# The place of the Hyena norm's sum on TensorE and of its roots on ScalarE at the start of the attention loop

## Chip, cores and metric

One core of one Trainium2 chip. The time is device microseconds from launch to end; the profile adds a span, from the first to the last instruction. Engines: PE (TensorE), DVE (VectorE), ACT (ScalarE), POOL (GpSimd), SP (which issues the DMAs).

## What is computed

Two layers of a hybrid backbone over 256 latent tokens and 256 context tokens of width 1024. In each layer one input projection feeds three mixers: a bidirectional state-space scan, attention (8 query heads, 2 key heads, head size 64), and a Hyena long convolution. Each mixer's result gets an RMS norm of its own, the three stand side by side and go through an output projection; then follows a SwiGLU block. What matters here are the Hyena norm and the attention:

```python
def _rmsnorm(t, g):
    y = t * lax.rsqrt(jnp.mean(t * t, axis=-1, keepdims=True) + EPS)
    return y * g

def _gqa(q, k, v):
    s = jnp.einsum('bqgrd,bkgd->bgrqk', q, k)
    pr = jax.nn.softmax(s, axis=-1)
    return jnp.einsum('bgrqk,bkgd->bqgrd', pr, v)

y_hy = _rmsnorm(x0 * _long_conv(v * x1, filt, bias), hy_norm_g)   # 512 channels
x = x + g1 * (concat([y_ssd, y_att, y_hy]) @ w_out)
```

Layer 0 works on latent and context tokens (512 columns, 16 pairs of heads and token tiles), layer 1 on the latent tokens alone (256 columns, 8 pairs).

## The kernel before, in words

Each engine has an instruction list of its own, written out by hand; semaphores tie them together. `p.sig(ins, name)` counts a semaphore up when the instruction is done, `p.after(name, k)` waits on this engine for k more counts, `p.own(name)` for all that this engine itself has made. An engine works its list in order, so what stands behind a wait waits too. Features lie on partitions (blocks of 128), tokens on columns; most products are split into high and low halves (L716 to L718).

The Hyena result lies in `yhy` as four blocks. Its norm needs the sum over all 512 channels for each token:

1. ACT squares the four blocks into `fsq` (L1671).
2. POOL adds block 1 to 0 and block 3 to 2 (L608), and signals `hy_added` twice.
3. PE multiplies both sums with a matrix of ones and accumulates them in the PSUM bank `other + 1` (L1270): the sum over partitions, repeated on all of them. It signals `hy_summed` twice.
4. ACT makes the factor (mean + eps)^(-1/2) as an exponential of a logarithm into `hrs` (L1658, L1659) and signals `hy_rms`.
5. DVE multiplies the four blocks of `yhy` with `hrs` (L2359), ACT rounds them with the gain into `f_hi` (L1682, behind the copies of pairs 1 and 2), DVE makes the low halves `hy_lo` (L2351, ahead of the divisions of pairs 1 and 2), and from the fourth pair on PE uses them for the parts of the output projection (`part_half(PARTS + h)`).

At the same time the attention runs over pairs i, as a loop through three engines:

- PE: `scores(i + 1)` (L1194, into banks 4 and 5), `attend(i - 1)` (L1228, L1233), `turn_probs(i)` (transpositions, L1209, into banks 6 and 7).
- DVE: `invert_sums(i)` (L2283), `row_max(i + 1)` (L2275), `divide(i - 1)` (L2300, L2301), its half of `copy_probs(i)` (L2291). For i = 0 the multiplication of step 5 (L2359) stands behind the copy, with its wait for `hy_rms`.
- ACT: `softmax(i + 1)` (exponentials, L1645), its half of `copy_probs(i)` (L1654).

`scores(i + 1)` overwrites the banks of `scores(i)`, so it waits for both exponentials of pair i (L1192). `attend(1)` uses the bank of the Hyena sum and waits for `hy_rms` (L1217). Ahead of the loop stand `scores(0)` and two halves of a part of the output projection (`part_half(6)`, `part_half(7)`), then the sum (L1268 to L1270); on ACT `softmax(0)`, then the roots (L1673, L1674).

SP loads the weight pieces through a ring of four buffers; each load waits until PE has used the piece four places earlier (L450).

Of the kernel before, what the change touches and what calls it, by code (L numbers as in the profile page):

```python
# [108 lines left out]
def part_banks(l):  # L109

    parts = 2 * ((PLAN[l, "out"][1] - 2) % 2)
    return parts, 2 - parts


def half_after(l, i):


    h = (i - 3) // 2 if l == 0 and i % 2 == 1 else i - 3 if l == 1 else -1
    return h if 0 <= h < PARTS - 3 else None
# [116 lines left out]
def backbone(nc, x, c, ctx_in, c_ctx, w_mod, b_mod, norm1_g, w_in, ssd_conv_w, ssd_conv_b, ssd_a_log,  # L236
# [3 lines left out]
    with ExitStack() as stack:  # L240
# [3 lines left out]
        def at(name, kb, shape, dt=F32):  # L244
            return nc.alloc_sbuf_tensor_at(name, [P] + shape, dt, offset=base + int(kb * KB))
# [82 lines left out]
        prod, fsq = at("prod", 40, [2, 512]), at("fsq", 40, [4, T])  # L328
# [5 lines left out]
        hrs, ars = at("hrs", 180, [T]), at("ars", 182, [T])  # L334
# [5 lines left out]
        ps = stack.enter_context(nc.psum_tensor("ps", [P, 8, 512], F32))  # L340
        MOD, STAT, ACC = 4, 5, 5
        ident, ones, trif, trib = (c_sq[:, i, :] for i in range(4))
# [77 lines left out]
        def tokens(l):  # L420
            return T if l == 0 else L
# [201 lines left out]
        def _(pe):  # L623
            mm, transpose = nc.tensor.matmul, nc.tensor.transpose
            p = Program(pe, "pe")
# [247 lines left out]
            for l in range(DEPTH):  # L873
                n = tokens(l)
# [199 lines left out]
                for ch, (kind, col, idx) in enumerate(W_IN):  # L1074
                    if ch < 2:
                        continue
                    i, q, s = g0 + 2 * ch, q0 + ch, 2 * ch
# [54 lines left out]
                parts, other = part_banks(l)  # L1132
# [5 lines left out]
                def part_half(h):  # L1138


                    i, j = h // 2, h % 2
                    if j == 0:
                        pe.wait_ge(w_lo_done, g0 + i + 1)
                    if i > 0:
                        p.after("part_read")
                    else:
                        pe.wait_ge(pair_free[parts // 2], (q0 - 2) // 2 + 1)
                    last = block_of(g0 + i, parts // 2, j, 4, n, lambda k: mixed(i // 4, k), True, True)
                    if j == 1:
                        last.then_inc(w_used, 1)  # L1150
                    else:
                        p.sig(last, "part_half")

                def turn_vx(t):

                    if t >= 2:
                        p.after("vn_ready")
                    for k in range(4):
                        last = transpose(ps[:, 6 + t % 2, k * P:(k + 1) * P], halves[t % 2][:, k, t // 2, :], ident)
                    p.sig(last, "vx_transposed")  # L1160
# [24 lines left out]
                def scores(i):  # L1185


                    t, b = i // 4, i % 4
                    t0 = 0 if t < 2 else 2
                    for j in range(2):  # L1190
                        if i > 0:
                            p.after("probs_ready")  # L1192
                        row = slice(64 * j, 64 * j + 64)
                        last = mm(ps[:, 4 + j, 0:(4 - t0) * P].rearrange("p (t k) -> p t k", k=P), qkT[row, t, b, :],  # L1194
                                  qkT[row, t0:4, 4, :], start=True, stop=True)
                    p.sig(last, "scores")

                def turn_probs(i):


                    nk = 4 if i // 4 < 2 else 2
                    if i == pairs - 1:
                        p.after("probs_ready", 2)
                    for j in range(2):
                        if i > 0:
                            p.after(("probT_act", "probT_dve")[j])
                        for kk in range(nk):
                            keys = slice(kk * P, (kk + 1) * P)
                            last = transpose(ps[:, 6 + j, keys], prob[:, i % 2, j, keys], ident)  # L1209
                        p.sig(last, "turned_psum")  # L1210

                def attend(i):


                    nk, v0 = (4, 0) if i // 4 < 2 else (2, 2)
                    if i == 1:
                        p.after("hy_rms")  # L1217
                    if i >= 2:
                        p.after("o_ready")
                    if i == pairs - 1:  # L1220
                        p.after("probT_act")
                        p.after("probT_dve")
                    else:
                        pe.wait_ge(S["probT_act"], PAIRS_BEFORE[l] + i + 1)
                        pe.wait_ge(S["probT_dve"], PAIRS_BEFORE[l] + i + 1)
                    for kk in range(nk):
                        for j in range(2):
                            mm(ps[64 * j:64 * j + 64, other + i % 2, 0:P], v_nat[:, v0 + kk, j * HD:(j + 1) * HD],  # L1228
                               probT[:, i % 2, j, kk * P:(kk + 1) * P], start=(kk == 0), stop=(kk == nk - 1))
                    p.after("rec_ready")  # L1230
                    c = 2 * (i % 4)
                    for j in range(2):
                        last = mm(ps[64 * j:64 * j + 64, other + i % 2, P:2 * P], sm[:, 2, c + j:c + j + 1].to_broadcast([P, HD]), ident,  # L1233
                                  start=True, stop=True)
                    p.sig(last, "pv_done")

                pairs = 4 * tiles
                turn_vx(0)
                turn_vx(1)
# [25 lines left out]
                scores(0)  # L1265
                part_half(6)
                part_half(7)
                for k in (0, 2):  # L1268
                    p.after("hy_added")
                    p.sig(mm(ps[:, other + 1, 0:n], ones, fsq[:, k, 0:n], start=(k == 0), stop=(k == 2)), "hy_summed")  # L1270

                for i in range(pairs):
                    if i + 1 < pairs:
                        scores(i + 1)
                    if i > 0:
                        attend(i - 1)
                    turn_probs(i)
                    h = half_after(l, i)
                    if h is not None:
                        if h == 0:  # L1280
                            p.after("hy_ready", 4)
                        part_half(PARTS + h)
# [10 lines left out]
                for ch in range(4):  # L1293
                    i = g0 + PARTS + ch
# [20 lines left out]
                for part, (c0, cnt) in enumerate(FFN):  # L1315
# [12 lines left out]
                    for f in range(1 - part, cnt):  # L1328
                        for r in range(4):
                            up, half = gate_up(part, f, r)  # L1330
                            i, q = g0 + 4 * f + r, q0 + 2 * f + up
# [11 lines left out]
                    for ch in range(4):  # L1343
                        for sub in range(3):
                            i = g0 + 3 * ch + sub
# [33 lines left out]
        def _(act):  # L1379
            A = nc.scalar.activation  # L1380
            p = Program(act, "act")
# [90 lines left out]
            for l in range(DEPTH):  # L1472
                n = tokens(l)
# [159 lines left out]
                other = part_banks(l)[1]  # L1633
# [3 lines left out]
                def softmax(i):  # L1637

                    keys = T if i // 4 < 2 else L
                    if i >= 2:  # L1640
                        act.wait_ge(S["turned_psum"], 2 * (PAIRS_BEFORE[l] + i - 1))
                    for j in range(2):
                        c = 2 * (i % 4) + j
                        p.after("row_max")
                        p.sig(A(prob[:, i % 2, j, 0:keys], ps[:, 4 + j, 0:keys], ACT.Exp, bias=sm[:, 0, c:c + 1],  # L1645
                                accum_out=sm[:, 1, c:c + 1]), "probs_ready")

                def copy_probs(i):

                    keys = T if i // 4 < 2 else L  # L1650
                    act.wait_ge(S["turned_psum"], 2 * (PAIRS_BEFORE[l] + i) + 1)
                    if i >= 2:
                        act.wait_ge(S["pv_done"], PAIRS_BEFORE[l] + i - 1)
                    p.sig(A(probT[:, i % 2, 0, 0:keys], ps[:, 6, 0:keys], ACT.Copy), "probT_act")  # L1654

                def norm_features(sums, root, name):

                    p.chain(A(root[:, 0:n], sums, ACT.Ln, scale=1.0 / 512, bias=eps1[:, 0:1]))  # L1658
                    p.sig(A(root[:, 0:n], root[:, 0:n], ACT.Exp, scale=-0.5), name)  # L1659
# [10 lines left out]
                for k in range(4):  # L1670
                    p.sig(A(fsq[:, k, 0:n], yhy[:, k, 0:n], ACT.Square), "hy_sq")  # L1671
                softmax(0)
                p.after("hy_summed", 2)  # L1673
                norm_features(ps[:, other + 1, 0:n], hrs, "hy_rms")  # L1674
                for i in range(4 * tiles):
                    if i + 1 < 4 * tiles:
                        softmax(i + 1)
                    copy_probs(i)
                    if i in (1, 2):
                        for k in (2 * i - 2, 2 * i - 1):  # L1680
                            p.after("hy_normed")
                            p.sig(A(f_hi[:, 8 + k, 0:n], yhy[:, k, 0:n], ACT.Identity, scale=vecT[:, l, V_HYG + k:V_HYG + k + 1]), "hy_hi")  # L1682
                    h = half_after(l, i)
                    if h is not None and h % 2 == 1:
                        round_w(g0 + PARTS // 2 + h // 2 + 2)
# [851 lines left out]
```

## Time and profile before

| | us |
|---|---|
| median of 3 runs | 1236.29 (1236.06 to 1238.84) |
| profiled execution | 1237.98 |
| its span | 1236.2 |
| PE busy in the span | 1197.3 |
| DVE busy | 821.7 |
| ACT busy | 522.9 |
| POOL busy | 12.5 |

A busy share is a mean over the whole span; what an edit at one place is worth is read from the order of time there, and from what ended the idle time of each engine. The place of the edit is from 314 us to 332 us in layer 0, and from 972 us to 989 us in layer 1.

### The profile page before, as it was taken

What the parts mean: (1) busy time and instruction counts of PE and PEld (TensorE: products, weight loads), DVE (VectorE), ACT (ScalarE), POOL (GpSimd) and SP (SyncE); (2) the same over time, 40 slices, a digit from 0 to 9 for tenths busy, and PEclk for the clock granted to TensorE, in tenths of its full rate; (3) what the DMA queues carried; (4) which work ended last, traced back from release to release, by engine and by line L of the source; (5) the groups of instructions that cost most, each with busy time, mean ns of one, the idle gap of its engine ahead of it and who ended that gap; (6) DMA issues with size and microseconds to landing.
All of it is one profiled execution on the core that took longest, in us unless ns stands there. A gap on an engine that the chain in (4) does not pass through costs nothing. (4 is left out here: it accounts for less than half of the span.)

```text
span 1236.2 us, 16708 instructions
## 1 busy us (share of the span) xinstructions
PE 1197.3 (97%) x6758; PEld 960.1 (78%) x6758; DVE 821.7 (66%) x1287; ACT 522.9 (42%) x907; POOL 12.5 (1%) x16
## 2 busy tenths in 40 slices
PE   6999999999999999999999999999999998999998
PEld 3666877777677788888887778678888688889888
DVE  5654357968767738777556656566599876776674
ACT  4452535452544433231122232346566545443454
POOL 0000000000100000000000000000000000000000
PEclk9999999999999999999999999999999999999999
DMA  9832343431012245555655454323344223655553
GB/s 339 270 118 89 118 139 97 163 98 53 19 34 60 68 164 172 187 203 189 189 197 199 143 195 153 94 68 108 100 117 120 69 69 103 199 186 183 186 182 122
DMA packets 132388, 171.82 MB, mean 139 GB/s; under 512 B 9268, under 2 KB 112342, under 8 KB 132312
## 3 DMA queue, kind: packets, MB, share of 16 engines
q1 hardware_dynamic: 131828, 170.58, 42.9%
q8 instruction: 53, 0.87, 0.3%
q10 hardware_dynamic: 484, 0.18, 0.1%
q14 instruction: 23, 0.19, 0.0%
HBM read 169.69 MB, written 1.05 MB: 138 GB/s over the span
## 5 line engine op out<-in xcount | busy, mean ns | idle before, releaser
L1829 DVE TENSOR_TENSOR w_lo<-w_raw,w_hi 128x1024 fp32r<-128x1024 f32 (+1 forms) x220 | 264.2, 1206 | 171.4 <-ACT w_hi L1456 169.6
L1456 ACT ACTIVATE w_hi<-w_raw 128x1024 fp32r<-128x1024 f32 (+1 forms) x220 | 228.2, 1042 | 333.8 <-DMA w_raw<-in_w_gu_dram 142.6
L716 PE MATMUL ps<-h_hi,w_hi 128*128 128x512 f32 (+1 forms) x576 | 218.7, 380 | 0.9 <-DVE w_lo L1829 0.3
L718 PE MATMUL ps<-h_hi,w_lo 128*128 128x512 f32 (+1 forms) x576 | 212.7, 369 | 0.0
L717 PE MATMUL ps<-h_lo,w_hi 128*128 128x512 f32 (+1 forms) x576 | 212.4, 369 | 0.0
L716 PE MATMUL ps<-f_hi,w_hi 128*128 128x512 f32 (+1 forms) x472 | 168.0, 356 | 2.8 <-DVE xT L2233 2.5
L718 PE MATMUL ps<-f_hi,w_lo 128*128 128x512 f32 (+1 forms) x472 | 162.7, 345 | 0.0
L716 PEld LDWEIGHTS ps<-h_hi,w_hi 128*128 128x128 f32 x576 | 108.5, 188 | 27.0 <-issue 9.1
L718 PEld LDWEIGHTS ps<-h_hi,w_lo 128*128 128x128 f32 x576 | 108.4, 188 | 18.8
L717 PEld LDWEIGHTS ps<-h_lo,w_hi 128*128 128x128 f32 x576 | 108.6, 189 | 17.4
L727 PE MATMUL ps<-h_hi,w_hi 128*128 128x512 f32 x320 | 113.2, 399 | 0.4 <-ACT gate L1761 0.4
L716 PEld LDWEIGHTS ps<-f_hi,w_hi 128*128 128x128 f32 x472 | 89.5, 190 | 19.7 <-issue 4.7
L718 PEld LDWEIGHTS ps<-f_hi,w_lo 128*128 128x128 f32 x472 | 89.5, 190 | 11.0
L717 PE MATMUL ps<-f_lo,w_hi 128*128 128x512 f32 (+1 forms) x240 | 90.1, 375 | 0.0
L728 PE MATMUL ps<-h_hi,w_lo 128*128 128x256 f32 x320 | 89.9, 281 | 0.0
L727 PEld LDWEIGHTS ps<-h_hi,w_hi 128*128 128x128 f32 x320 | 60.1, 188 | 15.5 <-DVE w_lo L1829 0.6
L728 PEld LDWEIGHTS ps<-h_hi,w_lo 128*128 128x128 f32 x320 | 60.4, 189 | 0.0
L717 PEld LDWEIGHTS ps<-f_lo,w_hi 128*128 128x128 f32 x240 | 45.2, 188 | 8.2 <-issue 0.5
L2451 DVE SCALAR_TENSOR_TENSOR m_acc<-m_odd,cact,m_acc 128x1024 f32<-128x1024 f32 x40 | 50.2, 1280 | 0.5
L1645 ACT ACTIVATE prob<-ps,sm 128x512 f32<-128x512 f32 (+1 forms) x48 | 29.1, 611 | 40.5 <-DVE sm L2275 38.0
L2414 DVE TENSOR_TENSOR hidden<-gate,ps 128x1024 f32<-128x1024 f32 (+1 forms) x12 | 14.1, 1176 | 42.6 <-PE ps L718 39.1
L1107 PE MATMUL ps<-w_hi,h_hi 128*128 128x512 f32 x96 | 40.8, 425 | 0.5 <-DVE xbc L2001 0.5
(345 smaller groups left out, 1912.3 us busy)
## 6 DMA issues: line engine op xcount, KB each, us to landing
w_raw<-in_w_gu_dram SPq DMA_DIRECT2D x88, 512.0 KB, 3.5
w_raw<-in_w_in_dram SPq DMA_DIRECT2D x60, 512.0 KB, 3.8
w_raw<-in_w_down_dram SPq DMA_DIRECT2D x32, 512.0 KB, 3.4
m_even<-in_w_mod_dram SPq DMA_DIRECT2D x14, 1024.0 KB, 5.8
m_odd<-in_w_mod_dram SPq DMA_DIRECT2D x14, 1024.0 KB, 5.7
m_raw<-in_w_mod_dram SPq DMA_DIRECT2D x24, 512.0 KB, 5.4
m_first<-in_w_mod_dram SPq DMA_DIRECT2D x16, 512.0 KB, 10.4
w_raw<-in_w_out_dram SPq DMA_DIRECT2D x16, 512.0 KB, 3.4
```

What stands on the lines that cost most here:

```text
L716: mm(o, w_hi[:, i % RING, w], hi[:, 0:n], start=first and k == 0, stop=False)
L717: mm(o, w_hi[:, i % RING, w], lo[:, 0:n], start=False, stop=False)
L718: last = mm(o, w_lo[:, i % RING, w], hi[:, 0:n], start=False, stop=final and k == nk - 1)
L727: mm(o, w_hi[:, i % RING, w], both(k), start=first and k == 0, stop=False)
L728: last = mm(o[:, 0:L], w_lo[:, i % RING, w], both(k)[:, 0:L], start=False, stop=final and k == nk - 1)
L1107: mm(o, h_hi[:, b, tok], w_hi[:, (i + half) % RING, w], start=(b == 0), stop=False)
L1456: A(w_hi[:, i % RING, w], w_raw[:, i % RING, w], ACT.Copy).then_inc(w_hi_done, 1)
L1645: p.sig(A(prob[:, i % 2, j, 0:keys], ps[:, 4 + j, 0:keys], ACT.Exp, bias=sm[:, 0, c:c + 1], accum_out=sm[:, 1, c:c + 1]), "probs_ready")
L1829: TT(w_lo[:, i % RING, w], w_raw[:, i % RING, w], w_hi[:, i % RING, w].bitcast(F32), ALU.subtract).then_inc(w_lo_done, 1)
L2414: TT(hidden[:, :, 0:n], gate[:, :, 0:n], ps[:, 2 * ((q + 1) % 2):2 * ((q + 1) % 2) + 2, 0:n], ALU.mult).then_inc(pair_free[(q + 1) % 2], 1)
L2451: ins = STT(out=acc, in0=src, scalar=by, in1=acc, op0=ALU.mult, op1=ALU.add)
```

## The change

On PE the sum moves from ahead of the loop to behind `turn_probs(0)`: it now stands behind `scores(1)` and the transpositions of the first pair, and ahead of `scores(2)`. On ACT the roots move from behind `softmax(0)` to behind `softmax(1)` and the copy of the first pair. DVE, POOL and SP keep their lists. No instruction is added or dropped.

```diff
+                def hyena_sum():
+
+                    for k in (0, 2):
+                        p.after("hy_added")
+                        p.sig(mm(ps[:, other + 1, 0:n], ones, fsq[:, k, 0:n], start=(k == 0), stop=(k == 2)), "hy_summed")
+
                 pairs = 4 * tiles
...
                 scores(0)
                 part_half(6)
                 part_half(7)
-                for k in (0, 2):
-                    p.after("hy_added")
-                    p.sig(mm(ps[:, other + 1, 0:n], ones, fsq[:, k, 0:n], start=(k == 0), stop=(k == 2)), "hy_summed")
-
                 for i in range(pairs):
                     if i + 1 < pairs:
                         scores(i + 1)
                     if i > 0:
                         attend(i - 1)
                     turn_probs(i)
+                    if i == 0:
+                        hyena_sum()
...
                 softmax(0)
-                p.after("hy_summed", 2)
-                norm_features(ps[:, other + 1, 0:n], hrs, "hy_rms")
                 for i in range(4 * tiles):
                     if i + 1 < 4 * tiles:
                         softmax(i + 1)
                     copy_probs(i)
+                    if i == 0:
+                        p.after("hy_summed", 2)
+                        norm_features(ps[:, other + 1, 0:n], hrs, "hy_rms")
```

## Rows read from the trace of the kernel before

**Rows 1.** The page, part 1: busy us (share of span), instructions

```profile
PE 1197.3 (97%) x6758; PEld 960.1 (78%) x6758; DVE 821.7 (66%) x1287; ACT 522.9 (42%) x907; POOL 12.5 (1%) x16
```

**Rows 2.** Order of time, PE, layer 0: start, duration, work [idle before, releaser]

```profile
314.14 1.99 PE L1270 MATMUL ps<-fsq,c_sq 128*128 128x512 f32 x4
316.06 1.13 PE L1194 MATMUL ps<-qkT 64*128 64x512 f32 x4
317.12 1.09 PE L1209 MATMUL ps<-c_sq,prob 128*128 128x128 f32 x8
318.79 1.79 PE L1194 MATMUL ps<-qkT 64*128 64x512 f32 x4 [0.58 <-ACT prob L1645]
320.51 1.09 PE L1228 MATMUL ps<-probT,v_nat 128*64 128x128 f32 x16
...
321.75 1.09 PE L1209 MATMUL ps<-c_sq,prob 128*128 128x128 f32 x8
323.24 1.79 PE L1194 MATMUL ps<-qkT 64*128 64x512 f32 x4 [0.39 <-ACT prob L1645]
```

**Rows 3.** Order of time, DVE, layer 0

```profile
316.26 0.16 DVE L2283 RECIPROCAL sm<-sm 128x2 f32<-128x2 f32 x1
317.23 1.29 DVE L2275 TENSOR_REDUCE sm<-ps 128x1 f32<-128x512 f32 x2 [0.81 <-PE ps L1194]
...
319.03 2.49 DVE L2359 TENSOR_TENSOR yhy<-yhy,hrs 128x512 f32<-128x512 f32 x4
321.56 0.17 DVE L2283 RECIPROCAL sm<-sm 128x2 f32<-128x2 f32 x1
321.64 1.27 DVE L2275 TENSOR_REDUCE sm<-ps 128x1 f32<-128x512 f32 x2
```

**Rows 4.** Order of time, ACT, layer 0

```profile
316.16 0.69 ACT L1658 ACTIVATE hrs<-ps,eps 128x512 f32<-128x512 f32 x1 [2.37 <-PE ps L1270]
316.88 0.63 ACT L1659 ACTIVATE hrs<-hrs 128x512 f32<-128x512 f32 x1
317.96 0.69 ACT L1645 ACTIVATE prob<-ps,sm 128x512 f32<-128x512 f32 x1 [0.45 <-DVE sm L2275]
...
319.30 0.59 ACT L1654 ACTIVATE probT<-ps 128x512 f32<-128x512 f32 x1
...
323.75 0.59 ACT L1654 ACTIVATE probT<-ps 128x512 f32<-128x512 f32 x1
324.22 1.33 ACT L1682 ACTIVATE f_hi<-yhy,vecT 128x512 fp32r<-128x512 f32 x2
```

**Rows 5.** Order of time, layer 1: one row of PE, then four of DVE

```profile
973.94 0.70 PE L1270 MATMUL ps<-fsq,c_sq 128*128 128x256 f32 x2 [0.78 <-POOL fsq L608]
...
975.14 0.16 DVE L2283 RECIPROCAL sm<-sm 128x2 f32<-128x2 f32 x1
975.75 1.29 DVE L2275 TENSOR_REDUCE sm<-ps 128x1 f32<-128x512 f32 x2 [0.45 <-PE ps L1194]
...
977.55 1.42 DVE L2359 TENSOR_TENSOR yhy<-yhy,hrs 128x256 f32<-128x256 f32 x4
...
979.13 1.29 DVE L2275 TENSOR_REDUCE sm<-ps 128x1 f32<-128x512 f32 x2
```

**Rows 6.** Order of time, ACT, layer 1

```profile
974.68 0.47 ACT L1658 ACTIVATE hrs<-ps,eps 128x256 f32<-128x256 f32 x1 [1.39 <-PE ps L1270]
975.18 0.42 ACT L1659 ACTIVATE hrs<-hrs 128x256 f32<-128x256 f32 x1
...
977.81 0.59 ACT L1654 ACTIVATE probT<-ps 128x512 f32<-128x512 f32 x1
```

**Rows 7.** Stretches: us, busy of PE, PEld, DVE, ACT, POOL, clock, DMA, GB/s

```profile
928.00:931.00 3.00, 1.43 (x13) 1.46 (x14) 2.93 (x8) 2.61 (x5) 0.00 (x0) 1.00 0.63 169
1021.84:1023.87 2.03, 0.00 (x0) 0.00 (x0) 1.98 (x3) 0.02 (x1) 0.00 (x0) 1.00 0.40 95
1023.88:1027.28 3.40, 2.96 (x10) 2.61 (x11) 1.73 (x3) 1.64 (x3) 0.00 (x0) 0.50 0.30 105
```

## The prediction

> **What bounds the kernel now.** I read the page's busy shares first: TensorE (PE) works for 1197.3 of 1236.2 us, so over the whole span it is the bound, and a change at one place counts only by the PE time that it opens or closes there [rows 1]. The edit touches one place per layer, the start of the attention loop, so the next view is the order of time there, engine by engine. In layer 0 PE runs the sum (1.92 us from its start to that of the next scores), scores of pair 1, the transpositions of pair 0, and then stands still for 0.58 us until ACT has made the second exponential; a pair later it stands for 0.39 us for the same reason [rows 2]. So here PE is not alone the bound. The reader should see a loop through three engines: PE's scores, the maximum on DVE, the exponential on ACT, back to PE for the scores that overwrite them. DVE shows the two facts that decide this case. It stands for 0.81 us until PE has made the scores of pair 1, because the sum stands ahead of them; and right behind the maximum and the copy of pair 0 it multiplies the Hyena blocks by the factors, 2.49 us, with no idle time before them, and only then takes the sums and the maximum of pair 2 [rows 3]. ACT had the factors ready long before: the logarithm started at 316.16 and the exponential ended at 317.51, while DVE reached the multiplication at 319.03 [rows 3, 4]. Today the factors are 1.5 us early.
>
> **The change part by part.** It adds and removes no instruction. The four matmul records of the sum go behind the eight transpositions of pair 0 on PE, and the two roots on ACT go behind the exponentials of pair 1 and the copy of pair 0. No DMA is issued by what moves and SP's queue keeps its order: the buffer release that SP waits for comes from the part ahead of the sum. POOL's two additions stay, and GpSimd is not waited for any more.
>
> First step, the gain at the front, layer 0. Scores of pair 1 start at 314.14 in place of 316.06 and end at 315.20 (they take 1.06) [rows 2]. DVE then finds them ready. Its reciprocal starts at 316.26, and where nothing is waited for the maximum follows 0.08 after the start of a reciprocal; so it starts at 316.34 in place of 317.23, 0.89 earlier [rows 3]. The other 1.03 of the 1.92 are lost at once, since DVE's own queue is now late. ACT follows: the exponentials of pair 1 start 0.89 earlier, and the copy of pair 0 at 318.41 in place of 319.30 [rows 4].
>
> Second step, the sum. PE does the transpositions from 315.20 to about 316.25 and the sum from there to 318.17 (1.92 again); the next scores could have started when the exponential comes, 318.79 - 0.89 = 317.90, so 0.27 of the sum show and the rest stands in a wait. The scores of pair 2 start at 318.17, 0.62 earlier than before [rows 2]. If it ended here, layer 0 would win 0.62.
>
> Third step, the wait that is made. The roots start behind the copy. An activation behind a copy starts 0.47 after the copy's start, so the logarithm starts at 318.41 + 0.47 = 318.88, when the sum is already there; logarithm to the end of the exponential takes 316.88 + 0.63 - 316.16 = 1.35, so the factors come at 320.23 [rows 4]. DVE reaches its multiplication 0.89 earlier than before, at 318.14, and now stands there for 2.1 us. With 0.03 for the handing over it starts at 320.26 in place of 319.03: **1.23 later** [rows 3]. Behind it in DVE's queue stand the reciprocal of pair 1, the maximum of pair 2, the division of pair 0 and the copy of pair 1. For the maximum of pair 2 waits ACT's exponential, for that PE's scores of pair 3 (323.24 before), and everything of the loop comes after them. The 0.62 of the second step is therefore given back, and 1.23 is lost. The wait of pair 1's attend for the factors on PE costs nothing: it comes after those scores.
>
> Layer 1 by the same working. The second matmul of the sum waited 0.78 for POOL and PE was free of it only at about 974.57, so scores come some 1.4 earlier, but DVE can use only 975.75 - (975.14 + 0.08) = 0.53 [rows 5]. Copy at 977.81 - 0.53 = 977.28, logarithm at 977.75, its 0.92 (975.18 + 0.42 - 974.68) end at 978.67, multiplication at 978.70 in place of 977.55, 1.15 later [rows 6]. The maximum of pair 2 follows by 1.42 + 0.12: 980.24 in place of 979.13, **1.11 later** [rows 5].
>
> Sum: 1.23 + 1.11 = 2.34 us slower, if PE's clock holds. Bounds: if the roots lose no time beyond their own durations behind the copy's start, the two steps are smaller by the 0.47 each (1.4 together); if they wait for the full 0.59 of the copy, larger by 0.12 each (2.6). I take 2.34, since 0.47 is read from the same pair of operations a little later [rows 4].
>
> **PE's clock** is the term that no row of the edit shows. In layer 0 PE has done the transpositions of pair 1 by about 322.84 - 0.62 = 322.2, and scores of pair 3 start at 323.24 + 1.23 = 324.47: a hole of 2.2 to 2.3 us where 0.39 was [rows 2]. In the trace of before, one stretch in the tail of layer 1 shows PE idle for 2.03 us at a granted clock of 1.00 and then 3.40 us at 0.50, that is at 1.2 in place of 2.4 GHz; in another PE was idle for 1.57 of 3.00 us and the clock stayed at 1.00 [rows 7]. The new hole is nearer to the first. The price there is at most 3.40 x 0.5 = 1.70 us, if PE is the late engine throughout; it is nothing if DVE and ACT are. In this loop they alternate, so I take half, 0.85, and keep 0 and 1.70 as ends. In layer 1 there was no hole at this place, so the new one is at most 0.53 + 1.11 = 1.64 us, like the stretch without a fall, and I give it nothing.
>
> [...]
>
> Against the profiled execution (1237.98 us, 1236.2 of it span) that makes 1237.98 + 2.34 + 0.85 = 1241.2. It stands 1.69 above the median of the runs, 1236.29, which is just what its half-clock stretch can cost; I carry the same difference to the median: 1236.29 + 3.19 = **1239.5 us**.
>
> **The rivals.** *The clock holds*: the hole is filled by nothing, but nothing is throttled: 1236.29 + 2.34 = 1238.6. For it speaks the 1.57 us stretch without a fall; against it that the new hole is longer. *Slower, a fall at both places*: PE falls to the low clock in the new hole and again in the tail of layer 1, as in the profiled execution; then 1237.98 + 3.19 = 1241.2, or up to 1242.0 at the full price of the first. It decides from the point where more than half of the executions fall in the tail, which one profile can't tell. *The gain stays*: the front gains 0.62 in layer 0 and 0.53 in layer 1, and nothing is given back because the multiplication isn't in the way of the maximum: 1236.29 - 1.15 = 1235.1. Against it: DVE's rows show the maximum directly behind the multiplication, and the program has it so. *The loss is absorbed downstream*: a wait for a weight load that doesn't move with the loop would hide it, 1236.3; but the loads of the output weights are themselves released by PE's work in the loop (L450), and so move with it. That the change doesn't do what it says is excluded: the order on each engine is written out by hand.
>
> **How the numbers follow.** Forecast (a fall in the new hole, at about half price) 0.40; clock holds 0.27; both falls 0.23; gain stays 0.04; absorbed 0.06. A measurement of this kernel tells about 0.3% from no change, 3.7 us here, so the border to slower is 1240.0. Faster by that much would need 1232.6, which no case gives: 0.01. Slower: both falls 0.23 and the part of the forecast in which the clock's price is over 1.4, 0.06, and a little for what I don't see: 0.30. Within: 0.69. The range takes the clock case without its low bound (1238.6 less the 0.9 of the smaller steps, 1237.7) up to both falls (1241.2), 1237.6 to 1241.4; below it lie the gain and the absorption, above it the full price of both.
>
> **What would show it.** Right: DVE's 0.81 and 0.45 us of waiting for the scores of pair 1 are gone, and it waits about 2.1 (layer 0) and 1.6 (layer 1) for ACT ahead of the multiplication by the factors; PE no longer waits for POOL; PE's 0.39 ahead of the scores of pair 3 becomes over 2 us; then, for a time, a granted clock of 0.5 in layer 0. From the exponentials of pair 1 to the maximum of pair 2 everything shows the shifts named above. Wrong: if DVE starts the multiplication without a wait for ACT, the third step fails; if the hole is there and the time is no longer, the loss was absorbed behind the loop.

## The result and the profile after

The changed kernel takes 1240.32 us (median of 22 runs, 1237.78 to 1243.38), the kernel before, measured beside it, 1236.62 us (22 runs, 1233.66 to 1240.19). The ratio is 1.0026, with a 95% interval of 1.0019 to 1.0034: a loss of some 3.2 us (3.7 us between the medians), about at the 0.3% that the prediction set as its border. The profiled execution has a span of 1240.1 us against 1236.2.

Order of time on PE, layer 0, kernel after (start, duration, work, and in brackets the idle time before and what ended it):

```profile
314.33 1.13 PE L1194 MATMUL ps<-qkT 64*128 64x512 f32 x4
315.39 1.09 PE L1209 MATMUL ps<-c_sq,prob 128*128 128x128 f32 x8
316.32 1.88 PE L1241 MATMUL ps<-fsq,c_sq 128*128 128x512 f32 x4
318.13 1.63 PE L1194 MATMUL ps<-qkT 64*128 64x512 f32 x4
...
324.55 2.74 PE L1194 MATMUL ps<-qkT 64*128 64x512 f32 x4 [2.53 <-ACT prob L1649]
```

The 0.58 us of waiting ahead of the scores of pair 2 [rows 2] is filled by the sum, as the change has it. In its place stands a hole of 2.53 us ahead of the scores of pair 3, where 0.39 us was. DVE shows where it comes from (layer 0, same columns):

```profile
316.36 0.16 DVE L2288 RECIPROCAL sm<-sm 128x2 f32<-128x2 f32 x1
316.43 1.27 DVE L2280 TENSOR_REDUCE sm<-ps 128x1 f32<-128x512 f32 x2
...
320.34 2.50 DVE L2364 TENSOR_TENSOR yhy<-yhy,hrs 128x512 f32<-128x512 f32 x4 [2.04 <-ACT hrs L1663]
...
322.96 1.27 DVE L2280 TENSOR_REDUCE sm<-ps 128x1 f32<-128x512 f32 x2
```

The maximum of pair 1 starts right behind the reciprocal; its 0.81 us of waiting [rows 3] is gone. But DVE then stands for 2.04 us until ACT has the factors, and the maximum of pair 2 follows only behind the multiplication. Everything in this trace lies 0.10 us later than in that of before (reciprocal 316.36 against 316.26), so the multiplication is 320.34 - 0.10 - 319.03 = 1.21 us later [rows 3]. ACT, layer 0, to be laid beside [rows 4]:

```profile
318.48 0.59 ACT L1658 ACTIVATE probT<-ps 128x512 f32<-128x512 f32 x1
318.95 0.70 ACT L1662 ACTIVATE hrs<-ps,eps 128x512 f32<-128x512 f32 x1
319.68 0.63 ACT L1663 ACTIVATE hrs<-hrs 128x512 f32<-128x512 f32 x1
```

In layer 1 the same picture on DVE, to be laid beside [rows 5] (this trace is there 978.62 - 975.14 = 3.48 us later at the reciprocal):

```profile
978.62 0.16 DVE L2288 RECIPROCAL sm<-sm 128x2 f32<-128x2 f32 x1
978.70 1.27 DVE L2280 TENSOR_REDUCE sm<-ps 128x1 f32<-128x512 f32 x2
...
982.18 1.43 DVE L2364 TENSOR_TENSOR yhy<-yhy,hrs 128x256 f32<-128x256 f32 x4 [1.62 <-ACT hrs L1663]
...
983.73 1.27 DVE L2280 TENSOR_REDUCE sm<-ps 128x1 f32<-128x512 f32 x2
```

The maximum of pair 2 is 983.73 - 3.48 - 979.13 = 1.12 us later than before.

Stretches of the kernel after (us, busy time of PE, PEld, DVE, ACT, POOL, granted clock, DMA share, GB/s): the hole of layer 0, what follows it, and the tail of layer 1 where the kernel before fell to the low clock [rows 7]:

```profile
321.90:324.30 2.40, 0.13 (x2) 0.00 (x0) 2.37 (x6) 0.58 (x1) 0.00 (x0) 1.00 0.00 0
324.36:331.18 6.82, 6.63 (x32) 4.56 (x32) 4.13 (x10) 4.43 (x12) 0.00 (x0) 0.50 0.02 5
...
1025.90:1029.00 3.10, 0.49 (x6) 0.29 (x4) 2.01 (x3) 1.02 (x3) 0.00 (x0) 1.00 0.58 195
1029.00:1033.00 4.00, 4.00 (x29) 3.90 (x30) 2.01 (x3) 1.92 (x5) 0.00 (x0) 1.00 0.10 35
```

With the end of the new hole PE's clock falls, and it runs 6.82 us at half clock. In the tail, where PE stood still as before, the clock stays up this time. So the two profiled executions can't simply be subtracted: 3.48 us are lost when the loop of layer 1 begins, another 1.1 in it, and some of it comes back in the tail by the fall that is missing there; the spans end 3.9 apart.

### The profile page after: what moved, and what is told of

Read it like the earlier page. It is cut to its first block and busy times, and to the rows that moved or that the text cites. A ratio compares the mean times of both kernels' runs of the same rounds, so it can differ in the third digit from the quotient of the medians.

```text
span 1240.1 us, 16708 instructions
## 1 busy us (share of the span) xinstructions
PE 1199.5 (97%) x6758; PEld 961.4 (78%) x6758; DVE 822.2 (66%) x1287; ACT 522.7 (42%) x907; POOL 12.8 (1%) x16
```

## The experiments

The theory (A): the factors come too late for DVE's queue, and what stands behind the multiplication there, the maximum of pair 2, carries the wait through ACT to PE; 1.2 us in layer 0, 1.1 in layer 1, and in layer 0 the fall of PE's clock on top. The rivals: the sum's new place on PE is what costs (D); only the roots' new place costs, and the sum's is a pure gain (E); all of it is the clock (C); the clock costs nothing (B).

**The wait taken away.** The changed kernel, with DVE's multiplication one step later, behind the maximum of pair 2. This moves the multiplication's own 2.49 us out of the way as well as the wait; the control for that is the pair of kernels with the multiplication on GpSimd, further down.

```diff
                     if i + 1 < pairs:
                         row_max(i + 1)
+                    if i == 1:
+                        p.after("hy_rms")
+                        for k in range(4):
+                            p.sig(TT(yhy[:, k, 0:n], yhy[:, k, 0:n], hrs[:, 0:n], ALU.mult), "hy_normed")
+                        p.own("hy_normed")
...
-                    if i == 0:
-                        p.after("hy_rms")
-                        for k in range(4):
-                            p.sig(TT(yhy[:, k, 0:n], yhy[:, k, 0:n], hrs[:, 0:n], ALU.mult), "hy_normed")
-                        p.own("hy_normed")
```

> The changed kernel, and on DVE the multiplication by the factors stands one step later: behind the reciprocal of pair 1 and the maximum of pair 2, ahead of the division of pair 0. Sum and roots stay where the change put them. Theory A: the wait for the roots no longer holds the maximum of pair 2; it starts at about 319.8 in layer 0 (322.96 in the changed kernel), PE's hole ahead of the scores of pair 3 is under 0.5 us, the clock stays up, and the loss is gone: before - 0.5 to before + 0.3. Rival D (the place of the sum on PE, between transpositions and scores of pair 2, is what costs): before + 2 or more, as in the changed kernel.

Measured: ratio to before 0.9998 (0.9988 to 1.0009), median 1235.93 us. DVE, then PE, of this kernel:

```profile
319.78 1.29 DVE L2280 TENSOR_REDUCE sm<-ps 128x1 f32<-128x512 f32 x2 [1.01 <-PE ps L1194]
320.99 2.49 DVE L2356 TENSOR_TENSOR yhy<-yhy,hrs 128x512 f32<-128x512 f32 x4
```

```profile
321.94 1.25 PE L1194 MATMUL ps<-qkT 64*128 64x512 f32 x4
324.87 1.09 PE L1228 MATMUL ps<-probT,v_nat 128*64 128x128 f32 x16 [1.68 <-DVE probT L2296]
```

Sum and roots stand where the change put them, and the loss is gone. The maximum of pair 2 starts 3.2 us earlier than in the changed kernel and waits only for the scores; the multiplication finds the factors there. Rival D falls. Nothing is won against before either: DVE's 2.49 us now stand ahead of the copy of pair 1, and PE waits 1.68 us for that, behind scores that came 1.4 us earlier than before (321.94 against 323.24 [rows 2], in a trace that is 0.08 late). DVE has as much to do as before, and here it is what PE waits for.

**One half of the change each.** First the roots alone, the sum as before:

```diff
                 softmax(0)
-                p.after("hy_summed", 2)
-                norm_features(ps[:, other + 1, 0:n], hrs, "hy_rms")
...
                     copy_probs(i)
+                    if i == 0:
+                        p.after("hy_summed", 2)
+                        norm_features(ps[:, other + 1, 0:n], hrs, "hy_rms")
```

> The kernel before with the second half of the change alone: the sum stays ahead of the loop on PE, the roots on ACT stand behind the exponentials of pair 1 and the copy of pair 0. Theory A: nothing is gained at the front and the factors come 0.47 + 1.35 us behind the start of the copy at 319.30: 321.12 in layer 0, 979.2 in layer 1, so the maximum of pair 2 is 2.1 and 1.6 us later; with a clock fall in layer 0 some 1 to 2 more: before + 3.7 to + 5.7. Rival D (the sum's place on PE costs): about before.

Measured: ratio 1.0043 (1.0027 to 1.0059), the highest of all, from five runs. On DVE:

```profile
317.08 1.29 DVE L2276 TENSOR_REDUCE sm<-ps 128x1 f32<-128x512 f32 x2 [0.82 <-PE ps L1194]
...
321.02 2.50 DVE L2360 TENSOR_TENSOR yhy<-yhy,hrs 128x512 f32<-128x512 f32 x4 [2.05 <-ACT hrs L1659]
...
323.63 1.27 DVE L2276 TENSOR_REDUCE sm<-ps 128x1 f32<-128x512 f32 x2
```

The wait for the scores of pair 1 is there as before, and the wait for the factors is added: the maximum of pair 2 is 323.63 + 0.15 - 321.64 = 2.14 us later (this trace is 0.15 early at the maximum of pair 1), where 2.1 was expected. Then the sum alone, the roots as before:

```diff
-                for k in (0, 2):
-                    p.after("hy_added")
-                    p.sig(mm(ps[:, other + 1, 0:n], ones, fsq[:, k, 0:n], start=(k == 0), stop=(k == 2)), "hy_summed")
                 for i in range(pairs):
...
                     turn_probs(i)
+                    if i == 0:
+                        hyena_sum()
```

> The kernel before with the first half of the change alone: the sum stands behind the transpositions of pair 0 on PE, the roots on ACT stay behind the exponentials of pair 0 and so ahead of those of pair 1. Theory A in its wider form (whoever stands in the loop behind the sum loses): ACT waits for the sum until about 318.2, the exponentials of pair 1 start at about 319.6 in place of 317.96, PE stands still about 2.3 us ahead of the scores of pair 2, and the loss is about 1.3 in layer 0 and 1.1 in layer 1, and up to 2 more by the clock: before + 2.4 to + 4.4. Rival E (only the roots' new place costs, the sum's new place is a pure gain): before - 1.1.

Measured: ratio 1.0034 (1.0021 to 1.0048). The sum's new place is no gain of itself (rival E falls): with the roots ahead of the exponentials of pair 1, it is now ACT that stands and waits for the sum, and PE for ACT. ACT and PE of this kernel, which is 1.4 us early in its trace:

```profile
316.70 0.69 ACT L1662 ACTIVATE hrs<-ps,eps 128x512 f32<-128x512 f32 x1 [4.35 <-PE ps L1241]
...
317.95 0.67 ACT L1649 ACTIVATE prob<-ps,sm 128x512 f32<-128x512 f32 x1
```

```profile
318.77 2.19 PE L1194 MATMUL ps<-qkT 64*128 64x512 f32 x4 [2.11 <-ACT prob L1649]
```

In both profiles the clock fell as well. First the roots alone, where the fall followed 2.53 us without work on PE, then the sum alone, where it followed the 2.11 us above:

```profile
325.99:332.82 6.83, 6.83 (x33) 4.42 (x34) 3.84 (x10) 4.50 (x10) 0.00 (x0) 0.50 0.02 4
```

```profile
320.04:323.45 3.41, 3.41 (x23) 2.24 (x22) 2.10 (x5) 1.45 (x4) 0.00 (x0) 0.50 0.01 2
```

So each half loses by itself, in another queue, and a part of each loss is the clock's. By the traces the two together lose less in layer 0 than the roots alone (the multiplication is 1.21 us later in place of 2.14), because the sum's place gives 0.9 us back at the front. The times don't settle this: the intervals of the ratios 1.0026 and 1.0043 overlap.

**The factors 0.47 us earlier.** The changed kernel with the roots ahead of the copy of pair 0:

```diff
                         softmax(i + 1)
-                    copy_probs(i)
                     if i == 0:
                         p.after("hy_summed", 2)
                         norm_features(ps[:, other + 1, 0:n], hrs, "hy_rms")
+                    copy_probs(i)
```

> The changed kernel with the roots on ACT one place earlier: behind the exponentials of pair 1 and ahead of the copy of pair 0. Theory A: the factors come 0.47 us earlier in both layers, DVE waits 0.47 less, the maximum of pair 2 is 0.76 and 0.64 us later than before; the copy of pair 0 comes 1.35 later, under PE's idle time. With a clock fall in layer 0 (the hole is still about 2 us): before + 1.4 to + 2.8. Rival D: as the changed kernel.

Measured: ratio 1.0015 (1.0002 to 1.0028). DVE in layer 0, where the reciprocal of pair 0 starts at 316.20, and in layer 1, where it starts at 975.52:

```profile
319.70 2.50 DVE L2364 TENSOR_TENSOR yhy<-yhy,hrs 128x512 f32<-128x512 f32 x4 [1.56 <-ACT hrs L1663]
...
980.14 1.27 DVE L2280 TENSOR_REDUCE sm<-ps 128x1 f32<-128x512 f32 x2
```

Set to the reciprocals of before, the multiplication is 0.73 later than before in layer 0 (expected 0.76), and the maximum of pair 2 0.63 in layer 1 (expected 0.64). DVE's wait fell from 2.04 to 1.56: it is the lateness of the factors that counts, to the tenth.

The clock did not do what was expected. PE's hole in layer 0 is cut in two, 0.60 us for the later copy and 1.37 us for the exponentials, and the granted clock stays at 1.00:

```profile
320.20 1.09 PE L1228 MATMUL ps<-probT,v_nat 128*64 128x128 f32 x16 [0.60 <-ACT probT L1658]
...
323.91 1.79 PE L1194 MATMUL ps<-qkT 64*128 64x512 f32 x4 [1.37 <-ACT prob L1649]
```

```profile
318.00:332.00 14.00, 11.51 (x97) 7.38 (x96) 11.37 (x25) 10.19 (x24) 0.00 (x0) 1.00 0.01 2
```

The two bare shifts add up to 1.36 us; measured are 1.7 us between the means, with a standard error of 0.7.

**One layer alone.** The change in layer 1, layer 0 as before (the same lines under `l == 1`):

> The change in layer 1 alone; layer 0 as before. Theory A: the maximum of pair 2 in layer 1 is 1.1 us later, PE's hole there is about 1.0 us and the clock stays up: before + 1.1. Rival C (the loss is the clock's, and so layer 0's alone): before within 0.3.

Measured: ratio 1.0009 (0.9995 to 1.0022), median 1236.78 against 1235.77 us. By the interval this is not told from no change, but the trace shows the shift:

```profile
973.48 0.16 DVE L2293 RECIPROCAL sm<-sm 128x2 f32<-128x2 f32 x1
...
977.04 1.43 DVE L2369 TENSOR_TENSOR yhy<-yhy,hrs 128x256 f32<-128x256 f32 x4 [1.62 <-ACT hrs L1665]
...
978.59 1.27 DVE L2285 TENSOR_REDUCE sm<-ps 128x1 f32<-128x512 f32 x2
```

From reciprocal to the maximum of pair 2 are 5.11 us, 3.99 before [rows 5]: 1.12 later, with a clock of 1.00 throughout the loop. The first product of the output projection inside the loop is still 1.10 later: 987.59 on PE, 14.11 us behind the reciprocal, against 988.15 and 13.01 before. That speaks against rival C, that all of the loss is the clock.

**The clock.** The changed kernel with two surplus matmuls, whose result no one reads, in PE's hole of layer 0; the first edit takes out a wait of PE for the factors in layer 0, which stands ahead of the surplus matmuls now:

```diff
-                    if i == 1:
+                    if i == 1 and l == 1:
                         p.after("hy_rms")
...
                     if i == 0:
                         hyena_sum()
+                    if (l, i) == (0, 1):
+                        p.after("hy_rms")
+                        for k in (0, 2):
+                            mm(ps[:, other + 1, 0:n], ones, fsq[:, k, 0:n], start=True, stop=True)
```

> The changed kernel with two surplus matmuls of 512 columns (as wide as the sum's, 1.88 us together, result unused) on PE in layer 0, in the 2.53 us that PE stands still ahead of the scores of pair 3; the order on all other engines is that of the changed kernel. Theory A (the factors' wait on DVE costs 1.2 us per layer, and on top of it the idle stretch throws PE to the low clock in layer 0): the wait and the shift of the maximum of pair 2 stay, the granted clock stays at 1.00 between 320 and 332 us, and the time falls by 1 to 2 us against the changed kernel, to about before + 2.3. Rival B (the clock's fall costs nothing because DVE and ACT set the pace there): the time stays at before + 3.2 to 3.7. Rival C (all of the loss is the clock): about before.

Measured: ratio 1.0025 (1.0015 to 1.0034), which can't be told from the changed kernel's 1.0026, though the trace did what theory A says. PE, and the stretch 320 to 332 us:

```profile
321.79 1.88 PE L1285 MATMUL ps<-fsq,c_sq 128*128 128x512 f32 x4
324.48 1.79 PE L1194 MATMUL ps<-qkT 64*128 64x512 f32 x4 [0.81 <-ACT prob L1653]
...
328.47 1.25 PE L1194 MATMUL ps<-qkT 64*128 64x512 f32 x4
```

```profile
320.00:332.00 12.00, 10.72 (x91) 6.80 (x88) 10.65 (x23) 7.74 (x18) 0.00 (x0) 1.00 0.01 3
```

The clock stays at 1.00. The scores of pair 4 (the last PE row) start at 328.47; before they did at 327.22, and this trace is 0.03 later (its reciprocal of pair 0 starts at 316.29): 1.2 us are left, the bare shift of layer 0. Because the times alone left the clock's price open, both kernels were run once more side by side.

> The changed kernel once more, beside the filled one on the same chip, because their two ratios (1.0026 and 1.0025) leave open what the fall of the clock costs on average. Theory A with the clock's price: before + 2.3 and, in the executions in which the clock falls in layer 0, up to 2.2 more; so a median of before + 3 to + 4, and 0.7 to 1.7 above the filled kernel. Rival B (the fall happens in too few executions or costs too little to show): the same time as the filled kernel, within 0.5.

> The filled kernel once more (the changed one with two surplus matmuls in PE's idle stretch of layer 0). Theory A with the clock's price: before + 2.3, 0.7 to 1.7 below the changed kernel of the same call. Rival B: the same time as the changed kernel, within 0.5.

Measured: the changed kernel 1240.97 us, ratio 1.0036 (1.0023 to 1.0050); the filled one 1238.68 us, ratio 1.0017 (1.0007 to 1.0027). The intervals still touch. Over both measurements, each set against the runs of the kernel before that were made beside it, the changed kernel is 3.3 us above the kernel before by the plain means (29 runs) and the filled one 2.3 (24 runs): 1.0 apart, with a standard error of 0.5. The granted clock that is on record for every run points the same way. Its mean is 0.9957 for the changed kernel, 0.9968 for the filled one and 0.9968 for 86 runs of the kernel before; over 1238 us this makes an estimated 0.0011 x 1238 / 0.5 = 2.7 us more at half clock in an average execution of the changed kernel. And rival C is out by the times too: the filled kernel kept its clock in layer 0 in both profiles, and both of its intervals lie above 1.

The new profile of the changed kernel shows a fall again, a shorter one. It began 1.69 us after PE had taken up its work again, at 323.67:

```profile
325.36:328.78 3.42, 3.42 (x26) 3.06 (x26) 3.10 (x6) 2.08 (x6) 0.00 (x0) 0.50 0.03 7
```

What a fall costs is read from the start of the scores of pair 3 to that of the scores of pair 5, behind the first products of the output projection in the loop. First and second profile of the changed kernel, then the filled kernel:

```profile
324.55:338.14 13.59, 13.14 (x77) 8.97 (x77) 8.51 (x19) 7.51 (x17) 0.00 (x0) 0.76 0.01 2
```

```profile
323.67:336.02 12.35, 11.91 (x77) 8.34 (x77) 8.49 (x19) 7.52 (x17) 0.00 (x0) 0.86 0.01 3
```

```profile
324.48:335.62 11.14, 10.51 (x76) 7.07 (x76) 8.30 (x19) 7.41 (x17) 0.00 (x0) 1.00 0.01 3
```

The first takes 2.45 us longer than the filled one, with 6.82 us at half clock in it, the second 1.21 us longer, with 3.42 us. So the fall costs about 0.36 us for each us. PE's busy time grew by 2.63 and 1.40 us, 0.39 and 0.41 for each us and not 0.5, and its idle time, 0.63 us in the filled kernel, shrank by 0.2.

**The multiplication off DVE.** If DVE's queue is the place, another engine for the multiplication should pay in both kernels. GpSimd takes it (the same lines in both; GpSimd now waits for `hy_rms`):

```diff
                 p.sig(add_block(2, 3), "hy_added")
+                p.after("hy_rms")
+                for k in range(4):
+                    p.sig(nc.gpsimd.tensor_tensor(yhy[:, k, 0:n], yhy[:, k, 0:n], hrs[:, 0:n], ALU.mult), "hy_normed")
...
-                    if i == 0:
-                        p.after("hy_rms")
-                        for k in range(4):
-                            p.sig(TT(yhy[:, k, 0:n], yhy[:, k, 0:n], hrs[:, 0:n], ALU.mult), "hy_normed")
-                        p.own("hy_normed")
```

> The changed kernel with the multiplication by the factors on GpSimd in place of DVE (GpSimd's additions of the same size take 1.3 to 2.2 us each). Theory A: no one in the loop waits for the roots any more, so the gain at the front stays (0.6 and 0.5 us), and DVE has 2.5 and 1.4 us less to do: the maximum of pair 2 starts when the scores are there, about 319.8 in layer 0. Before - 1.5 to before - 2.8, with no fall of the clock. Rival D: slower than before. If the multiplications on GpSimd come too late for the rounding on ACT (they have until about 322 and 326 us), the time is before + 1 or more.

> The kernel before with the multiplication by the factors on GpSimd in place of DVE: the control for the run above. Theory A: in layer 0 the maximum of pair 2 starts about 1.0 us earlier (320.6), the scores of pair 3 0.5, and the gain is 0.5 to 1.5; in layer 1 PE is the bound there and nothing is gained. Before - 0.5 to before - 1.5. The difference to the run above is then what the changed places of sum and roots are worth when no one waits for the factors: about 1.1.

> The changed kernel with the multiplication by the factors on GpSimd once more, as the candidate that is faster than both kernels: before - 1 to before - 2.8, ratio 0.998 to 0.999 with an upper end under 1.

Measured: the changed kernel so 0.9984 (0.9973 to 0.9996), and once more 0.9983 (0.9973 to 0.9993); the kernel before so 0.9988 (0.9977 to 1.0000). The changed kernel so is faster than both kernels, and than the kernel before by some 2 us. With the multiplication off DVE the change no longer loses anything, though sum and roots stand where it put them: between the two kernels lie 0.6 us in favour of the changed one, with a standard error of 0.6, where the change by itself loses some 3.2 us. This is the control for the first experiment. The expected gain of 1.1 us is neither shown nor excluded. POOL and DVE of the changed one say where a part of it goes:

```profile
321.03 4.96 POOL L616 TENSOR_TENSOR yhy<-yhy,hrs 128x512 f32<-128x512 f32 x4 [5.35 <-ACT hrs L1666]
```

```profile
320.44 1.29 DVE L2283 TENSOR_REDUCE sm<-ps 128x1 f32<-128x512 f32 x2 [1.01 <-PE ps L1197]
...
325.09 2.11 DVE L2359 SCALAR_TENSOR_TENSOR hy_lo<-yhy,vecT,f_hi 128x512 fp32r<-128x512 f32 x2
```

The maximum of pair 2 waits for the scores alone. But with the late roots GpSimd works until 326.0, and the two low halves on DVE take 2.11 us from the first start to the last end in place of 1.41. No wait is recorded between them, and the blocks and roundings that they read were done before. It is one instruction that lasts longer, 1450 ns. In the kernel before with the multiplication on GpSimd, which is through at 322.0, all four take about 745 ns (duration min/median/max; first and last start):

```profile
L2359 DVE SCALAR_TENSOR_TENSOR hy_lo<-yhy,vecT,f_hi x2: 740/1095/1450, 325.1 to 326.5; 128x512 fp32r<-128x512 f32 x2
```

```profile
L2354 DVE SCALAR_TENSOR_TENSOR hy_lo<-yhy,vecT,f_hi x4: 742/744/750, 324.7 to 329.1; 128x512 fp32r<-128x512 f32 x4
```

Counted from the reciprocal of pair 0 (317.00 and 315.70), the scores of pair 4 come 0.92 us earlier in the changed kernel (326.05 against 325.67), but PE's next work, which waits for the copy behind the low halves, comes only 0.21 earlier (328.48 against 327.39). So 0.7 us of the front's gain in layer 0 go to the longer low half. That GpSimd's work is what stretches it is argued from their standing side by side, in both profiles of this kernel; no run tests it by itself.

## Why the prediction was right

Forecast 1239.5 us, 3.2 above the median shown; measured a ratio of 1.0026, 3.2 us, and a median of 1240.32 us, 3.7 above the 1236.62 of the 22 runs beside it. By its own steps:

- *Front.* The maximum of pair 1 was to start 0.89 us earlier in layer 0. It starts at 316.43 - 0.10 = 316.33 against 317.23 [rows 3]: 0.90.
- *Sum.* PE was to be through with it at 318.17, so that 0.62 us stay. The scores of pair 2 start at 318.13 - 0.10 = 318.03 [rows 2]: 0.76. The sum took 1.81 us to the next start in place of 1.92. In layer 1 the scores of pair 1 were to come some 1.4 us earlier; they come 1.9 earlier (976.15 - 3.48 = 972.67 against 974.57), since the first half of the sum left their way too. It changes nothing, because DVE could use only 0.53 of it.
- *The wait made.* DVE was to wait 2.1 and 1.6 us for the factors; it waits 2.04 and 1.62. Multiplication 1.23 later in layer 0: 1.21. Maximum of pair 2 1.11 later in layer 1: 1.12. The last term there was taken as 1.42 + 0.12 = 1.54 us behind the multiplication, where the rows of before have 1.58; it took 1.55. The sum of both layers, 2.34, agrees with the filled kernel: 2.3 us in the mean of its runs with an error of 0.3, 3.1 and 2.1 by its two ratios.
- *The way to the end.* The wait went on through the exponentials to the scores of pair 3 and was not absorbed behind the loop; with the multiplication out of the way, behind the maximum or on GpSimd, all of the loss was gone.
- *The clock.* That the new hole brings a fall was right in both profiles. Its size was the weak term: 0.85 us were taken, half of the most that a fall of 3.40 us could cost. A fall of that length cost 1.21, and one was twice as long (6.82 us, 2.45), over the upper end of 1.70 that the prediction kept. The runs give 1.0 us in the mean, with an error of 0.5, so that 0.85 came near the average partly by luck. The row that it was taken from was read short, too: the 2.03 us are the idle time up to the fall, and PE stood still for 2.48 in all, 0.45 of it inside the 3.40 us at half clock.

```profile
1024.32 2.08 PE L755 MATMUL ps<-sqr,c_sq 128*128 128x256 f32 x4 [2.48 <-ACT sqr L1406]
```

- *The rival of both falls* did not describe the profile: the fall in the tail came in the trace of before and not in that of after, with about the same idle time there. It was read as a property of the kernel and is one of the execution: of the 13 profiles here 4 show it. The rivals of a gain that stays and of an absorbed loss are out; that the clock holds is out for both profiles.

## What to carry to other kernels

When work is moved into another engine's wait, look for who reads its result, and for what stands behind that reader in its queue. The sum filled a wait of 0.58 us on PE, but its consumer on DVE stood ahead of the next step of the loop, so the slack of the factors (1.5 us) was the price to compare with, not the wait that was filled. Either let the consumer stand behind the step that the loop needs, or give it to an engine outside the loop.

A change that opens a hole on TensorE can cost more than the hole: here 1.2 to 2.5 us more in the profiles in which the clock fell.

## What the runs showed of the hardware

- The granted clock fell to half (1.2 in place of 2.4 GHz) at the new hole of layer 0 in all four profiles in which PE stood still there for 2.1 to 2.5 us in one piece (2.53 in three, 2.11 in one). The fall began anywhere from 0.19 us before PE's next work to 1.69 us after it, and lasted 3.4 us in two profiles and 6.8 in two. In the tail PE stands still for 2.5 to 2.6 us in all 13 profiles, and the clock fell in 4 of them (after 2.48 in that of before, not after 2.60 in the first of the changed kernel). So the length of the idle time alone does not tell whether the clock falls, nor for how long. The Trainium skill, "TensorE: Matmul & The Clock Gate", section "What's actually happening", says that the throttled state is the default and that activity releases it; both profiles of the filled kernel agree, in which 1.88 us of useless matmuls in the hole kept the clock at 1.00.
- GpSimd multiplies four blocks of 128 x 512 in 4.96 us, 1.24 each, where DVE takes 2.49. Beside it DVE's work on `ps` (the maximum 1.29, the copy 0.69) and ACT's rounding (1.33 for two) last no longer than elsewhere, but a low half on DVE, which reads `yhy` and `f_hi`, lasted 1.45 in place of 0.74 us.
